# Opening order, the rotary angles' place, and tokens-first layer values in a two-block kernel on one core

## The chip, the core and the metric

The kernel runs on one core of a Trainium2 chip. The metric is the device time of one execution in microseconds (us). TensorE (PE in the profile), VectorE (DVE), ScalarE (ACT), GpSimd (POOL) and SyncE (SP, which here only issues DMAs) each run their own list of instructions in order and meet at semaphores.

## What is computed

The reference is a stack of two models over 512 tokens of width 1024. The first has two layers; each mixes tokens by differential attention and by a gated linear recurrence, followed by an MLP and a gate. The second block (a Mamba layer and an attention layer with 256 context tokens) is not touched by the change except for the names of some semaphores. The part of a first-block layer that matters here:

```python
hn = rms_norm(h, g_mix[l])
proj = hn @ w_in[l]                       # 1024 x 2560
q, k, v, xr, gr = jnp.split(proj, [A, 2 * A, 3 * A, 3 * A + R], axis=-1)
q = partial_rope(q.reshape(B, S, N_DIFF_HEADS, 2, DIFF_HEAD_DIM), positions)
k = partial_rope(k.reshape(B, S, N_DIFF_HEADS, 2, DIFF_HEAD_DIM), positions)
v = v.reshape(B, S, N_DIFF_HEADS, V_HEAD_DIM)
...
o = diff_attention(q, k, v, lam)
xc = causal_depthwise_conv(xr, conv_w[l], conv_b[l])
y = rg_lru(xc, w_gate_a[l], b_gate_a[l], w_gate_x[l], b_gate_x[l], lru_lambda[l])
y = y * jax.nn.gelu(gr)
h = h + jnp.concatenate([o, y], axis=-1) @ w_out[l]
```

## The kernel before

**Weights.** All large weights come as one stream of tiles of 128 x 2048 float32 (1 MB, `wstream`). SP fetches them into two slots `wraw`. GpSimd splits each tile into a rounded high part `whi` (four TENSOR_SCALAR of 128 x 512, line 352) and a rest `wlo` (four TENSOR_TENSOR, line 356). It starts on tile k when tile k has landed and TensorE is done with tile k-2 (semaphore `tile_done`, which starts with two credits), and signals `wsplit`. Tiles 0 and 1 are split "by pieces" (lines 336 and 338): a quarter of `whi`, the same quarter of `wlo`, and a semaphore `w_piece` for each quarter, so that TensorE may begin on a tile that is partly split.

**Products.** `tile()` (line 384) multiplies one tile: for both halves m of its 256 output features and all eight blocks kb of the contraction it issues three products (`whi` by `uhi`, `wlo` by `uhi`, `whi` by `ulo`), where `uhi` and `ulo` are the high part and rest of the activations times the norm's gain. One tile is 48 products of 128 x 512 (line 400). Results stand features by tokens in PSUM. The division by the root mean square is done after the product: VectorE's `mix_out(j)` (line 1642) multiplies tile j's result by `rstd` into `proj`. The layer's ten input tiles are 0, 1 for `xr`, 2, 3 for `gr`, 4, 5 for Q, 6, 7 for K, and 8, 9 for V. A tile's PSUM banks are free again when `mix_out` of the tile two before is done.

**Norm.** ScalarE squares h, VectorE adds (line 1604), TensorE sums over features in the middle of tile 1 (`norm_sum(1)`), ScalarE takes the root, and VectorE the reciprocal (`norm_recip`, line 1612).

**Opening, layer 0.** SP fetches `posi` (positions, one row broadcast to 128 partitions), `misc`, `lpall` (the parameters), and weight tile 0; ScalarE fetches the first half of h, and its second half after the parameters. VectorE waits for the semaphore `cst` (all three of SP's first DMAs), computes the rotary angles (eight instructions, lines 1549 to 1556), one small product, the eight `ulo` blocks (line 1595), the sums of squares, and then `lru_rates`: seventeen instructions on 128 x 4 or 128 x 8 numbers (`softplus` at lines 2353 to 2361 and lines 1579 to 1582), each waiting for the one before. ScalarE has supplied their input (lines 1058 and 1059, after a table load) and takes the sine of the angles after its squares (`rotary`). Then come `norm_recip(1)` and `mix_out(0)`.

**Middle.** VectorE runs mix_out(0), `lambdas` (three small instructions), the convolution of blocks 0 and 1, mix_out(1), blocks 2 and 3, mix_out(2), mix_out(3). TensorE then does the gates' products (line 475), tiles 4 to 7, and the recurrence runs on ScalarE and VectorE beside them, with `mix_out(4)` to `mix_out(7)` in between.

**Values and rotations.** After tile 7 TensorE issues four rotations of Q (`rope`, line 488, a float32 product of a 512-token block with a permutation, two instructions each), tiles 8 and 9, four rotations of K, and then turns V from features by tokens to tokens by features with sixteen 128 x 128 transposes (line 502), since attention needs V as [tokens, features]. VectorE finishes each rotation with three instructions (lines 1711, 1713, 1716). ScalarE copies V to `vtok` (line 1152). The attention loop runs over 16 units of (head, query block): scores on TensorE (lines 517 and 519), maximum on VectorE (line 1736), exponentials on ScalarE (line 1160), `combine` on VectorE (lines 1746 to 1751), transposes and products with V on TensorE. GpSimd meanwhile splits the tile two ahead of the last one finished.

## Time and profile before

| what | value |
|---|---|
| median of the runs | 2647.99 us |
| lowest and highest of three runs | 2640.88 and 2651.42 us |
| the profiled execution's own time | 2651.38 us |
| its span (first to last instruction) | 2649.6 us |
| TensorE busy in it | 2452.4 us, 93% |
| VectorE, GpSimd, ScalarE busy | 54%, 49%, 30% |
| mean granted TensorE clock | 0.963 of full |

The first row is what a change is measured against; the third and fourth belong to the one execution that the trace shows. A share near 93% for TensorE is a busy time with idle gaps around single places, which the views by wait and in order of time show.

### The profile page before, as it was taken

To read this page: it belongs to the slowest core of one execution; us is meant where nothing else is said; L and a number is where in the kernel's file an instruction comes from. 1 tells how busy PE (TensorE), PEld (TensorE's weight loads), DVE (VectorE), ACT (ScalarE), POOL (GpSimd) and SP (SyncE) were. 2 spreads that over 40 slices of the span, in tenths; PEclk is the share of its full clock that TensorE was granted. 3 is DMA by queue.
4 is the path that set the end of the run, shared out by engine and by line. 5 is a ranking of instruction groups with operands and counts; after the bars stand their busy time and mean duration, and the time that the engine had idled before them with its cause. 6 is when DMAs were issued, how large, how long until landed. Compare 5 with 4: busy or idle time off the path is not lost.

```text
span 2649.6 us, 35776 instructions
## 1 busy us (share of the span) xinstructions
PE 2452.4 (93%) x13296; PEld 2042.8 (77%) x13296; DVE 1443.6 (54%) x1778; ACT 798.3 (30%) x1705; POOL 1302.2 (49%) x1204
## 2 busy tenths in 40 slices
PE   6989999999998899999977699999999997998997
PEld 5657888888765688888855688988988886876776
DVE  8564311133766441111336787887888887326762
ACT  2233210112232420011214334334333333325771
POOL 6734766767774276666752243442443431263003
PEclk9989999999998999999998899999999997899999
DMA  4210344343221034434221011111110111121001
GB/s 151 80 48 32 113 142 143 127 135 104 80 80 64 18 104 141 137 129 140 95 102 64 32 49 47 47 39 40 47 47 32 47 54 68 47 81 48 1 1 48
DMA packets 33688, 199.27 MB, mean 75 GB/s; under 512 B 4400, under 2 KB 6576, under 8 KB 13616
## 3 DMA queue, kind: packets, MB, share of 16 engines
q1 hardware_dynamic: 22896, 159.93, 17.5%
q10 hardware_dynamic: 10688, 37.83, 4.4%
q8 instruction: 80, 1.31, 0.2%
q14 instruction: 24, 0.20, 0.0%
HBM read 192.50 MB, written 5.24 MB: 75 GB/s over the span
## 4 chain that ended last, share of the span: by engine, by line
PE 75%; DVE 16%; issue 5%; ACT 3%; POOL 1%; DMA 0%; DVEq 0%; ACTq 0%; SPq 0%; POOLq 0%
PE ps L400 39%; PE ps L653 11%; PE ps L890 5%; DVE convd L1918 3%; PE ps L771 2%; PE ps L749 1%; PE ps L622 1%; PE ps L788 1%; PE ps L971 1%; PE ps L425 1%; PE ps L517 1%; PE ps L988 1%; DVE convd L1932 1%; PE ps L596 1%; PE ps L758 1%
## 5 line engine op out<-in xcount | busy, mean ns | idle before, releaser
L352 POOL TENSOR_SCALAR whi<-wraw 128x512 fp32r<-128x512 f32 x592 | 403.7, 709 | 1312.2 <-PE ps L653 568.8
L356 POOL TENSOR_TENSOR wlo<-wraw,whi 128x512 fp32r<-128x512 f32 x592 | 882.2, 1519 | 0.0
L400 PE MATMUL ps<-uhi,whi 128*128 128x512 f32 x960 | 384.5, 400 | 31.3 <-DVE ulo L1595 16.2
L400 PE MATMUL ps<-uhi,wlo 128*128 128x512 f32 x960 | 377.2, 393 | 0.0
L400 PE MATMUL ps<-ulo,whi 128*128 128x512 f32 x960 | 376.8, 392 | 0.0
L653 PE MATMUL ps<-inhi,whi 128*128 128x384 f32 (+1 forms) x784 | 249.4, 353 | 31.1 <-ACT raw L1291 17.0
L400 PEld LDWEIGHTS ps<-uhi,whi 128*128 128x128 f32 x960 | 182.5, 190 | 78.3 <-issue 28.3
L653 PE MATMUL ps<-inhi,wlo 128*128 128x384 f32 (+1 forms) x784 | 237.6, 338 | 0.0
L653 PE MATMUL ps<-inlo,whi 128*128 128x384 f32 (+1 forms) x784 | 237.4, 338 | 0.0
L1770 DVE TENSOR_TENSOR h<-h,ps 128x1024 f32<-128x1024 f32 x40 | 48.9, 1221 | 307.3 <-PE ps L400 307.3
L400 PEld LDWEIGHTS ps<-uhi,wlo 128*128 128x128 f32 x960 | 182.5, 190 | 38.7 <-issue 1.9
L400 PEld LDWEIGHTS ps<-ulo,whi 128*128 128x128 f32 x960 | 182.2, 190 | 38.6
L400 PE MATMUL ps<-hidhi,whi 128*128 128x512 f32 x512 | 202.2, 395 | 0.0
L400 PE MATMUL ps<-hidhi,wlo 128*128 128x512 f32 x512 | 199.5, 390 | 0.0
L400 PE MATMUL ps<-hidlo,whi 128*128 128x512 f32 x512 | 199.2, 389 | 0.0
L653 PEld LDWEIGHTS ps<-inhi,whi 128*128 128x128 f32 (+1 forms) x784 | 146.1, 190 | 38.4 <-issue 29.5
L1364 ACT ACTIVATE ebuf<-ps,tabg 128x128 f32<-128x128 f32 x384 | 104.2, 383 | 163.5 <-PE ps L760 112.9
L1789 DVE SCALAR_TENSOR_TENSOR hm<-ps,rstd 128x1024 f32<-128x1024 f32 x32 | 39.2, 1224 | 203.2 <-PE ps L400 203.2
L653 PEld LDWEIGHTS ps<-inhi,wlo 128*128 128x128 f32 (+1 forms) x784 | 146.4, 190 | 2.4
L653 PEld LDWEIGHTS ps<-inlo,whi 128*128 128x128 f32 (+1 forms) x784 | 145.8, 189 | 0.9
L1918 DVE SCALAR_TENSOR_TENSOR convd<-raw,cpg,convd 128x770 f32<-128x770 f32 x128 | 142.6, 1114 | 2.3
L1203 ACT ACTIVATE hsq<-hm 128x1024 f32<-128x1024 f32 x32 | 34.0, 1062 | 294.2 <-DVE hm L1789 294.2
(389 smaller groups left out, 4594.8 us busy)
## 6 DMA issues: line engine op xcount, KB each, us to landing
wraw<-in_wstream SPq DMA_DIRECT2D x150, 1024.0 KB, 4.8
modraw<-in_modw ACTq DMA_DIRECT2D x48, 512.0 KB, 3.6
hspill<-hres ACTq DMA_DIRECT2D x1, 3072.0 KB, 8.7
hback<-hspill ACTq DMA_DIRECT2D x1, 3072.0 KB, 10.2
h<-in_x ACTq DMA_DIRECT2D x2, 1024.0 KB, 7.0
out<-hfin SPq DMA_DIRECT2D x2, 1024.0 KB, 3.9
gw<-in_gates ACTq DMA_DIRECT2D x2, 512.0 KB, 4.7
pT<-in_pT ACTq DMA_DIRECT2D x2, 512.0 KB, 4.0
```

Of the source, the lines that this page charges most:

```text
L352: pool.tensor_scalar(whi[:, s, c], wraw[:, s, c], 1.0, 0.0, ALU.mult, ALU.add).then_inc(wraw_read, 1)
L356: ins = pool.tensor_tensor(wlo[:, s, c], wraw[:, s, c], whi[:, s, c].bitcast(F32), ALU.subtract)
L400: mm = pe.matmul(ps[:, 2 * bank + m, :], a[:, w, c:c + P], b[:, kb, :], start=(n == 0 and i == 0), stop=(n == KB - 1 and i == 2))
L425: mm = pe.matmul(ps[32 * j:32 * j + 2, 5, 0:P], cvec[:, kb, :], modraw[:, kb, :], start=(half == 0), stop=(half == 1))
L653: mm = pe.matmul(ps[0:width, q + half, 0:HALF], a[:, s, c:c + width], b[:, kb, half * HALF:(half + 1) * HALF], start=(n == 0), stop=(n == ...
L771: mm = pe.matmul(ps[:, 6, d * 256:(d + 1) * 256], ck[:, c * P:(c + 1) * P], ast[:, slot, :], start=True, stop=True)
L890: mm = pe.matmul(ps[:, q + m, :], a[:, k % 2, c:c + P], b[:, kb, t0:t0 + S], start=(kb == 0 and i == 0), stop=(kb == KB - 1 and i == 2))
L1203: A(hsq[n % 2][:, :, :], hm[n % 2][:, :, :], ACT.Square).then_inc(L["sqh_r"], 1)
L1364: ins = A(ebuf[:, d, r, :], ps[:, 4 + d, r * P:(r + 1) * P], ACT.Exp, bias=tabg[:, K_NB + 2 * c + d, r:r + 1])
L1770: V.tensor_tensor(h[:, 2 * j:2 * j + 2, :], h[:, 2 * j:2 * j + 2, :], TWO(bank), ALU.add).then_inc(L["h_r"], 1)
L1789: V.scalar_tensor_tensor(out=hm[n % 2][:, :, :], in0=TWO(n % 2), scalar=0.0, in1=rstd2, op0=ALU.max, op1=ALU.mult).then_inc(L["m_r"], 1)
L1918: ins = V.scalar_tensor_tensor(out=o, in0=r[:, n:n + CW], scalar=cpg[:, 6 * b + n:6 * b + n + 1], in1=o, op0=ALU.mult, op1=ALU.add)
```

## The change

It has two parts. **Opening:** SP fetches `misc` and `lpall` first and waits for them alone; `posi` comes after weight tile 1, which itself now waits for tile 0 to land; VectorE computes the recurrence's rates (`lru_rates`) before the `ulo` blocks; the angles and the casts of two constants move into layer 0's recurrence, behind line 1688's instruction and ahead of mix_out(5); ScalarE's sines follow there; four weight tiles are split by pieces instead of two. `mix_out(1)` stands ahead of all four convolution blocks, and `lambdas` behind mix_out(3). **Values:** tiles 8 and 9 are multiplied with the activations as the stationary operand and the weights as the moving one, 96 products of 128 x 256 for a tile, so that V comes out tokens first; the sixteen transposes and mix_out(8) and mix_out(9) are gone. As the tokens are now on partitions, `rstd` is needed as a column: `rate_columns` turns it with four one-column products, and ScalarE applies it while it copies V. The rotations are issued in pairs: ahead of tile 8, in its middle, between the tiles, and in the middle of tile 9. The rest of the diff renames semaphores and moves buffers.

```diff
+FIRST = 4
...
     @block.sync
-        sp.dma_start(posi[:, :], io["positions"].partition_broadcast(P)).then_inc(cst, 16)
         sp.dma_start(misc[:, :], io["consts"][:, 256:272]).then_inc(cst, 16)
         sp.dma_start(lpall[:, :, :], io["lparams"]).then_inc(cst, 16)
         sp.dma_start(wraw[:, 0, :], io["wstream"][0]).then_inc(wland[0], 16)
-        sp.wait_ge(cst, CST)
+        sp.wait_ge(wland[0], 16)
         sp.dma_start(wraw[:, 1, :], io["wstream"][1]).then_inc(wland[1], 16)
+        sp.dma_start(posi[:, :], io["positions"].partition_broadcast(P)).then_inc(cst2, 16)
...
     @block.gpsimd
-        for s in range(2):
-            pool.wait_ge(wland[s], 16)
-            pool.wait_ge(tile_done, s + 1)
+        for k in range(FIRST):
+            s = k % 2
+            pool.wait_ge(wland[s], 16 * (k // 2 + 1))
+            pool.wait_ge(tile_done, k + 1)
...
     @block.tensor
-            for m in range(Q0, Q0 + 4):
+            def rate_columns():
+                pe.wait_ge(L["rstd_r"], l * PER["rstd_r"] + 1)
+                pe.wait_ge(L["gate_t"], l * PER["gate_t"] + 8)
+                for t in range(4):
+                    mm = pe.matmul(ps[:, 5, t:t + 1], rstd[:, t * P:(t + 1) * P], ident[:, 0:1], start=True, stop=True)
+                mm.then_inc(L["rcol_ps"], 1)
+
+            def values_tile(j, midway):
+                w = (l * LAYER_TILES + NFM + j) % 2
+                tile_wait(l, NFM + j)
+                banks_wait(j, (L["v_r"], l * PER["v_r"] + 2 * j + 2))
+                for t in range(4):
+                    for kb in range(KB):
+                        for i, (a, b) in enumerate(((uhi, whi), (uhi, wlo), (ulo, whi))):
+                            mm = pe.matmul(ps[:, 2 * j + t // 2, t % 2 * TM:(t % 2 + 1) * TM], a[:, kb, t * P:(t + 1) * P],
+                                           b[:, w, kb * TM:(kb + 1) * TM],
+                                           start=(kb == 0 and i == 0), stop=(kb == KB - 1 and i == 2))
+                    if t == 1:
+                        mm.then_inc(L["v_ps"], 1)
+                        midway()
+                mm.then_inc(tile_done, 1)
+
+            def ropes(m):
                 rope(m)
-            for j in range(8, 10):
-                pair(j)
-            for m in range(K0, K0 + 4):
-                rope(m)
-
-            for t in range(4):
-
-                pe.wait_ge(L["proj_r"], l * PER["proj_r"] + 10)
-                for hd in range(HEADS):
-                    mm = pe.transpose(ps[:, t, hd * P:(hd + 1) * P], proj[:, V0 + hd, t * P:(t + 1) * P], ident[:, :])
-                mm.then_inc(L["v_ps"], 1)
+                rope(m + 1)
+
+            ropes(Q0)
+            rate_columns()
+            values_tile(0, lambda: ropes(Q0 + 2))
+            ropes(K0)
+            values_tile(1, lambda: ropes(K0 + 2))
...
     @block.scalar
-            for t in range(4):
-                act.wait_ge(L["v_ps"], l * PER["v_ps"] + t + 1)
-                A(vtok[:, t, :], ps[:, t, :], ACT.Copy).then_inc(L["v_r"], 1)
+            act.wait_ge(L["rcol_ps"], l * PER["rcol_ps"] + 1)
+            A(small[:, 56:60], ps[:, 5, 0:4], ACT.Copy).then_inc(L["rcol_r"], 1)
+            act.wait_ge(L["rcol_r"], l * PER["rcol_r"] + 1)
+            for j in range(2):
+                for half in range(2):
+                    act.wait_ge(L["v_ps"], l * PER["v_ps"] + j + 1) if half == 0 else tile_wait(NFM + j)
+                    for t in (2 * half, 2 * half + 1):
+                        ins = A(vtok[:, t, j * TM:(j + 1) * TM], ps[:, 2 * j + half, t % 2 * TM:(t % 2 + 1) * TM],
+                                ACT.Copy, scale=small[:, 56 + t:57 + t])
+                    ins.then_inc(L["v_r"], 1)
...
     @block.vector
             if l == 0:
                 lambda_products(0)
+                lru_rates(0)
                 for j in range(4):
                     rest(1, j, C_GMIX)
             for j in range(1, 4):
                 add_squares(1, j, sqn[j - 1])
-            if l == 0:
-                lru_rates(0)
...
             mix_out(0)
-            lambdas()
-            dve.wait_ge(L["proj_r"], l * PER["proj_r"] + 1)
-            conv(0)
-            conv(1)
             mix_out(1)
             dve.wait_ge(L["proj_r"], l * PER["proj_r"] + 2)
-            conv(2)
-            conv(3)
+            for b in range(4):
+                conv(b)
             mix_out(2)
             mix_out(3)
+            lambdas()
...
+            if l == 0:
+                angles()
             mix_out(5)
```

How the order of instructions moves on VectorE, at the very start of the program (`angt` are the angles, `small` the recurrence's parameters; line numbers are those of each kernel). Before:

```order
L1549 CAST angt_109<-posi 128x512
L1550 TENSOR_SCALAR angt_109<-angt_109,misc 128x512
L1551 TENSOR_SCALAR angt_110<-angt_109 128x512
L1552 TENSOR_SCALAR angt_110<-angt_110 128x512
L1554 SCALAR_TENSOR_TENSOR angt_109<-angt_110,angt_109 128x512 x3
L1556 TENSOR_SCALAR angt_109<-angt_109 128x512
L1573 TENSOR_TENSOR small<-lpall 128x2
L1595 SCALAR_TENSOR_TENSOR ulo<-h,lpall,uhi 128x512 x8
L1604 TENSOR_TENSOR acc_66<-acc_66,sqn_94 128x1024
L1604 TENSOR_TENSOR acc_66<-acc_66,sqn_95 128x1024
L1604 TENSOR_TENSOR acc_66<-acc_66,sqn_96 128x1024
```

And of the changed kernel at the same place:

```order
L1605 TENSOR_TENSOR small<-lpall 128x2
L2375 TENSOR_SCALAR small<-small 128x4
L2376 RECIPROCAL small<-small 128x4
L2377 TENSOR_TENSOR small<-small 128x4
...
L2381 SCALAR_TENSOR_TENSOR small<-small 128x4 x6
L2382 SCALAR_TENSOR_TENSOR small<-small 128x4
L2383 TENSOR_SCALAR small<-small 128x4
...
L1614 TENSOR_SCALAR small<-lpall 128x8
L1627 SCALAR_TENSOR_TENSOR ulo<-h,lpall,uhi 128x512 x8
L1636 TENSOR_TENSOR acc_66<-acc_66,sqn_94 128x1024
```

The angles are gone from here, and the seventeen small instructions stand ahead of the `ulo` blocks, on which TensorE's first product waits.

TensorE from the end of tile 7 to attention's first scores; `rperm` marks rotations, `ident,proj` the transposes of V, `proj` alone the scores. Before:

```order
L400 MATMUL ps<-uhi,wlo 128x512
L400 MATMUL ps<-ulo,whi 128x512
L488 MATMUL ps<-proj,rperm 128x512 x4
L400 MATMUL ps<-uhi,whi 128x512
L400 MATMUL ps<-uhi,wlo 128x512
L400 MATMUL ps<-ulo,whi 128x512
...
L400 MATMUL ps<-ulo,whi 128x512
L488 MATMUL ps<-proj,rperm 128x512 x4
L502 MATMUL ps<-ident,proj 128x128 x16
L517 MATMUL ps<-proj 128x128 x2
L519 MATMUL ps<-maskb,identb 128x128 x2
```

Changed (`ident,rstd` are the rate columns, `whi,uhi 128x256` the tokens-first products):

```order
L401 MATMUL ps<-ulo,whi 128x512
L489 MATMUL ps<-proj,rperm 128x512 x2
L496 MATMUL ps<-ident,rstd 128x1 x4
L507 MATMUL ps<-whi,uhi 128x256
L507 MATMUL ps<-wlo,uhi 128x256
L507 MATMUL ps<-whi,ulo 128x256
...
L489 MATMUL ps<-proj,rperm 128x512 x2
...
L489 MATMUL ps<-proj,rperm 128x512 x2
...
L489 MATMUL ps<-proj,rperm 128x512 x2
...
L507 MATMUL ps<-whi,ulo 128x256
L537 MATMUL ps<-proj 128x128 x2
L539 MATMUL ps<-maskb,identb 128x128 x2
```

K's rotations no longer stand behind both value tiles: two pairs of rotations now stand in the middle of a tile's products, and the scores follow the last product of tile 9 directly.

## Rows read from the trace of the kernel before

**Rows 1.** TensorE's waits from 0 to 235 us: total us, times, longest

```profile
...
PE ps L400 <- DVE ulo L1595: 16.2, 1, 16.2
...
PE ps L517 <- DVE proj L1716: 5.2, 1, 5.2
PE ps L400 <- POOL wlo L356: 4.4, 1, 4.4
PE ps L400 <- DVE proj L1642: 4.4, 1, 4.4
```

**Rows 2.** DMA issues from 0 to 30 us: KB each, us from issue to landing

```profile
...
gw<-in_gates ACTq DMA_DIRECT2D x1, 512.0 KB, 3.6
...
posi<-in_positions SPq DMA_DIRECT2D x1, 256.0 KB, 5.9
...
lpall<-in_lparams SPq DMA_DIRECT2D x1, 63.0 KB, 6.0
```

**Rows 3.** ScalarE in order of time, the opening: start us, us, instructions [idle before]

```profile
...
8.12 1.28 ACT L1058 ACT_TABLE_LOAD   x1 [8.12 <-DMA lpall<-in_lparams]
...
9.65 0.20 ACT L1059 ACTIVATE small<-small 128x4 f32<-128x4 f32 x1
...
36.99 0.69 ACT L1095 ACTIVATE rstd<-ps,misc 128x512 f32<-128x512 f32 x1 [10.93 <-PE ps L412]
```

**Rows 4.** VectorE in order of time, the opening

```profile
...
14.90 11.01 DVE L1595 SCALAR_TENSOR_TENSOR ulo<-h,lpall,uhi 128x512 fp32r<-128x512 f32 x8
...
32.66 0.16 DVE L2355 TENSOR_TENSOR small<-small 128x4 f32<-128x4 f32 x1
...
33.05 0.60 DVE L2357 TENSOR_SCALAR small<-small 128x4 f32<-128x4 f32 x1
33.69 5.44 DVE L2359 SCALAR_TENSOR_TENSOR small<-small 128x4 f32<-128x4 f32 x6
...
42.34 3.35 DVE L1612 RECIPROCAL rstd<-rstd 128x512 f32<-128x512 f32 x1
```

**Rows 5.** GpSimd in order of time: the weight splits

```profile
...
10.20 0.68 POOL L336 TENSOR_SCALAR whi<-wraw 128x512 fp32r<-128x512 f32 x1 [9.75 <-DMA wraw<-in_wstream]
...
33.01 2.38 POOL L352 TENSOR_SCALAR whi<-wraw 128x512 fp32r<-128x512 f32 x4 [0.62 <-POOL wlo L338]
35.35 5.01 POOL L356 TENSOR_TENSOR wlo<-wraw,whi 128x512 fp32r<-128x512 f32 x4
...
95.77 5.03 POOL L356 TENSOR_TENSOR wlo<-wraw,whi 128x512 fp32r<-128x512 f32 x4
...
160.03 6.72 POOL L356 TENSOR_TENSOR wlo<-wraw,whi 128x512 fp32r<-128x512 f32 x4
```

**Rows 6.** VectorE in order of time: end of the convolution, and mix_out(5)

```profile
...
60.50 2.78 DVE L1650 SCALAR_TENSOR_TENSOR xc<-proj,lpall,xc 128x511 f32<-128x511 f32 x3
...
102.11 1.23 DVE L1642 TENSOR_TENSOR proj<-ps,rstd 128x1024 f32<-128x1024 f32 x1 [7.37 <-PE ps L400]
```

**Rows 7.** The chain that ended last: full-size products, start us, us

```profile
...
47.10 24.42 PE ps L400 x96
...
135.30 21.79 PE ps L400 x96
```

**Rows 8.** TensorE in order of time: first rotations, first scores

```profile
...
129.82 1.88 PE L488 MATMUL ps<-proj,rperm 128*128 128x512 f32 x4
...
169.37 0.80 PE L517 MATMUL ps<-proj 64*128 64x128 f32 x4 [5.24 <-DVE proj L1716]
```

**Rows 9.** The chain that ended last: tokens-first products of the second block

```profile
...
2289.34 17.27 PE ps L872 x144
```

**Rows 10.** Line 846: one-column float32 products, ns min/median/max, first and last start

```profile
...
L846 PE MATMUL ps<-ones,sq x96: 165/352/352, 2246.2 to 2262.6; 128*128 128x1 f32 x96
```

**Rows 11.** VectorE in order of time: the last rotation, the fourth score maximum

```profile
...
167.22 0.68 DVE L1711 SCALAR_TENSOR_TENSOR rtmp<-ps,ropeS 128x512 f32<-128x512 f32 x1
...
176.58 1.23 DVE L1736 TENSOR_REDUCE small<-ps 128x2 f32<-128x1024 f32 x1 [0.53 <-PE ps L519]
```

More of the change, by code:

```diff
@@ L46 @@
 NLP = 63
-XR, GR, Q0, K0, V0 = 0, 4, 8, 12, 16
+XR, GR, Q0, K0 = 0, 4, 8, 12
+NFM = 8
 CTX = 256
```

95 lines of the change are left out of this document (45 added, 50 removed).

## The prediction

> **What bounds the kernel now.** I read the page of the profile first: TensorE is busy 93% of the span (the table above), so only time in which it stands idle, or work of its own, is worth anything. The view of TensorE's waits over the first 235 us then names the places in layer 0: 16.2 us until the first `ulo` block, 5.2 us before attention's first scores until the last rotation is added, 4.4 us on GpSimd's split of tile 7, and 4.4 us on `mix_out(0)` [rows 1]. Layer 1 has the same wait before the scores. Third, the timelines show what is late at each. In the opening VectorE sits until `lpall` has landed at 7.7 us [rows 2, 3], then spends the time to 14.90 on the angles and one small product before the first `ulo` [rows 4]; later TensorE awaits `mix_out(0)`, because the small instructions of `lru_rates` still run when the root is done (36.99 + 0.69, [rows 3]), and the reciprocal starts only at 42.34 [rows 4]. Ahead of attention all four rotations of K and the transposes follow tile 9: from the first rotation at 129.82 to the first scores at 169.37 are 39.6 us [rows 8], of which VectorE's last rotations are the end.
>
> **The cost of VectorE beside GpSimd** decides both parts. The small instructions take 0.16 us alone (line 2355, [rows 4]) but 0.60 while GpSimd runs `whi` and, inside the six of line 2359, up to 1.2 us while it runs `wlo`: from 33.05 on VectorE finished eight small instructions in just the 7.4 us in which GpSimd ran its eight [rows 4, 5]. So beside a split each small VectorE instruction costs one GpSimd instruction, 0.92 us on average, and about 1.0 where the split goes by pieces and has gaps; alone about 0.2 with its semaphore. The Trainium skill (page "SBUF — State Buffer", section "Who interferes with whom") says the same as a rule: VectorE with two SBUF inputs, or in a two-port mode, and GpSimd take their shared port pair in turn, each for a whole instruction. By that rule the move of the rates to where GpSimd begins its first tile speaks against the change, and it prices them as the rows do, at one GpSimd instruction each; were there no such turn-taking, the opening below would gain 7 us instead of 1.4.
>
> **Values, for each of two layers.** TensorE's new work between tile 7 and the scores: eight rotations, 1.88 us for two [rows 8], 7.5 us; 192 products of 128 x 256, for which the second block's tokens-first tile is the same form, 17.27 us for 144, 0.120 us each [rows 9], 23.0 us; four one-column products, eight instructions at 0.17 us start to start (16.4 us for 95) [rows 10], 1.4 us. Sum 31.9. The products themselves get dearer, 23.0 for 21.8 us [rows 7]; what is saved are the transposes, the waits within the rotations, and above all the tail. Is VectorE in time? The last rotation takes it 2.1 us with GpSimd idle (167.22 to the scores at 169.37, [rows 8, 11]); beside a split, where each of the two instructions without PSUM may wait for one of GpSimd's, I estimate 3.3. The last two are issued in the middle of tile 9, 5.8 us of products before its end, when the split of the next tile is nearly over: 4.1 to 6.6 us of work, so it ends 1.7 us before to 0.8 us after TensorE; I take 0.3 us of cost. ScalarE's last copies of V and a table load (1.28 us, [rows 3]) now follow the last product; the first exponentials can start some 2.2 us behind the scores' start, about when the first maxima are there. Gross gain: 39.6 - 31.9 = 7.6, less 0.3.
>
> What comes back: GpSimd's split of tile 11 starts when tile 9 is done. Before, it ran out under the last rotations (until 166.8, [rows 5]) and attention had GpSimd idle. Now tile 9 ends where the scores start, so about 7.4 us of split lie on attention's first units. `combine` of unit 0 has three instructions that take from SBUF, and each waits for a `wlo` (5.01 / 4 = 1.25 us) where it ran in 0.2 to 0.35: 2.7 us. The fourth maximum, which started 7.2 us behind the first scores (176.58 - 169.37, [rows 8, 11]), had waited 0.53 for TensorE [rows 11]; that much is slack. So 2.1 us; if the maxima, which read PSUM, and the reciprocals are blocked too it is 4; below it is 0, if GpSimd is the one who yields. The same section of the Trainium skill has reductions never contend; by it the 2.1 stand, and no row here shows it either way. Net per layer 7.6 - 0.3 - 2.1 = 5.2, bounds 3 and 7.6. Two layers: 10.4, from 6 to 15.
>
> **Opening.** Behind TensorE's first product at S come tiles 0 and 1 with the norm's sum (26.4 us, up to 42.7), then the 4.4 us wait, then tiles 2 and 3 in 24.42 us, where the same 96 products take 21.79 elsewhere: 2.6 us for slow products after the idle time [rows 1, 7]. With the rates gone from between, the norm's chain is: the root at S + 20.8 (36.99 - 16.2) and 0.7 long, reciprocal 3.4 [rows 3, 4], mix_out(0) 1.2, thus S + 26.1, before tile 1 ends. Both the 4.4 and the 2.6 go: 7.0 us gained, if S stays at 16.2. But S moves. `lpall` landed at 1.67 + 6.0 = 7.7, `posi` at 0.75 + 5.9 = 6.65 ahead of it in the same queue [rows 2]. Without `posi` it lands between 4.8 (issued at 1.2, and 3.6 us, the quickest landing in the opening, [rows 2]) and 7.2 (as long as before); I take 5.8. ScalarE then needs 2.1 us (7.7 to 9.85, [rows 3]) for the rates' input: 7.9. GpSimd began at 10.20 when weight tile 0 had landed [rows 5]; with 256 KB less ahead of it I put it at 9.0. About five of the seventeen instructions run free, twelve beside the split at 1.0: the rates end near 20.7, the first `ulo` (1.2 us there) at 21.8. S is 5.6 later and the opening gains 7.0 - 5.6 = 1.4 us. With `lpall` at 4.8 nearly eleven run free and S is near 16 (gain 7); with 7.2 all are beside the split and S is near 26 (loss 3). Weight tile 1 is fetched only after tile 0 has landed; GpSimd needs it 8 us later, the fetch takes about 7: nothing. Splitting tiles 2 and 3 by pieces lets TensorE start early on them, but tile 2's split (S + 13.3 to S + 21.5) and tile 3's first piece are ready anyway: nothing.
>
> **Moved work taken as hidden.** The angles with one small product took 7.2 us in the opening (7.7 to 14.9), partly beside a split [rows 2, 4]; they go into 7.37 us in which VectorE awaited tile 5 [rows 6]; GpSimd's `wlo` of tile 6 runs there (95.77 to 100.8, [rows 5]) and would end about 1 us later, 0.5 before it is needed; mix_out(5) up to 3 us later, which frees a bank for tile 7, 10 us on. The recurrence behind it shifts by as much, on whose overlap the 4.4 us wait for tile 7's split rests; I charge 0.3. Without that cover the angles would cost 3 us. The four convolutions in a row behind mix_out(1) end 1 to 2 us ahead of tile 3 by my count of turns, where they had 8 us of room (60.50 + 2.78 against 47.10 + 24.42, [rows 6, 7]): nothing, but each us beyond is one on the gates. ScalarE's sines with their table load lie in its wait for the scan.
>
> **Sum.** 10.4 + 1.4 - 0.3 = 11.5 us; as S has more room below than above I round to 12.5. The profiled execution took 2651.38 us, 3.4 above the median of the runs; off the median that makes 2635.5 us.
>
> **Rivals.** (a) *Both parts run free of GpSimd*: the parameters land near 4.8 and attention is not held up. For it: without `posi` only 71 KB stand ahead of the weights. Against it: the small instructions and the splits take turns plainly [rows 4, 5]. 7 + 15 = 22 us, 2626. (b) *The rates cost all that they free*: S at 26, opening loses 3 us, values at the low end or 5 each: 3 to 8 us, 2642. For it: `lpall`'s landing may hang on the fetch of h, which is as large as before. (c) *Slower:* the loading of the stationary operand sets the pace, since a layer now loads 192 of them for 96. If a 128 x 256 product takes the 0.227 us of a 128 x 512 one (21.79 / 96, [rows 7]), a layer pays 192 x 0.107 = 20.6 us more; the sum turns into 29 us lost, 2677. It decides, for 0.5% slower, from 0.18 us on. Against it stands the same form in the same kernel [rows 9]. (d) *No effect:* the waits merely change their name (attention's start held by the last rotation instead, 5 us, and S later by 7): 2647.
>
> **Chances.** Forecast (gain 8 to 17) 0.50, (a) 0.22, (b) 0.18, (c) 0.03, (d) 0.07. A measurement of this kernel tells about 0.5%, 13.2 us, from no change. Of the forecast's 0.50 half lies beyond that, and (a): faster 0.47. The other half, (d), and (b) but for 0.02: same 0.48. (c), and 0.02 of (b) where the angles or convolutions come out dearer besides: slower 0.05. Range: from just below (a), 2622, to (b)'s upper side, 2646; this leaves out a little of (a), and (c) and (d), some 0.15. It is as wide as the two unknown bounds (S, and attention beside the split) make it.
>
> **What the profile after will show.** TensorE's first product at 21.8 us (16: the rates ran free; 26: none did), and small VectorE instructions of about 1 us beside GpSimd's pieces. No wait of TensorE on mix_out(0). Tokens-first products 0.12 us apart. First scores 32 us behind tile 7's end in both layers, and line 1736's fourth maximum 9 us behind them, with GpSimd's `wlo` beside. A wait of the gates on the convolution, or of tile 6 or 7 on a later split than before, would make the forecast too good.

## The result, and the profile after

The changed kernel takes 2627.42 us (median of 6 executions, 2622.64 to 2629.79), the kernel before 2644.94 on the same chip (6 executions, 2640.26 to 2652.94): 0.9927 of it, 95% interval 0.9908 to 0.9947. It is faster by 17.5 us, 0.7%, where 12.5 were forecast, in a band of 8 to 17. The forecast time, 2635.5, was counted from the 2647.99 known then, and the measured one is 8.1 below it: 5.0 for the larger gain, 3.1 because the median before came out lower with more executions. The profiled execution of after took 2622.64 us, span 2620.8, granted clock 0.969.

The view of TensorE's waits over the first 235 us, to be laid beside [rows 1]:

```profile
...
PE ps L401 <- DVE ulo L1627: 18.1, 1, 18.1
PE ps L547 <- DVE patt L1777: 7.9, 6, 2.3
...
PE ps L537 <- ACT pexp L1188: 2.0, 3, 1.2
...
PE ps L401 <- POOL wlo L357: 0.2, 1, 0.2
```

and of before, two lines of the same view on the waits inside attention:

```profile
...
PE ps L527 <- DVE patt L1751: 5.6, 5, 2.1
...
PE ps L517 <- ACT pexp L1160: 0.8, 2, 0.4
```

The wait on mix_out(0) is gone (L401 <- DVE proj), as forecast. The 4.4 us wait for tile 7's split is down to 0.2, which was not. The 5.2 us before the scores is gone. Inside attention the waits have grown, from 5.6 to 7.9 us on `patt` and from 0.8 to 2.0 on `pexp`. The first product waits 18.1 us; 21.8 were forecast.

The opening, in order of time, ScalarE, GpSimd, VectorE, to be laid beside [rows 3 to 5]:

```profile
...
6.40 1.28 ACT L1078 ACT_TABLE_LOAD   x1 [6.40 <-DMA lpall<-in_lparams]
...
7.93 0.20 ACT L1079 ACTIVATE small<-small 128x4 f32<-128x4 f32 x1
```

```profile
...
8.55 0.62 POOL L337 TENSOR_SCALAR whi<-wraw 128x512 fp32r<-128x512 f32 x1 [8.10 <-DMA wraw<-in_wstream]
9.26 1.27 POOL L339 TENSOR_TENSOR wlo<-wraw,whi 128x512 fp32r<-128x512 f32 x1
10.49 0.62 POOL L337 TENSOR_SCALAR whi<-wraw 128x512 fp32r<-128x512 f32 x1
```

```profile
...
8.17 0.17 DVE L2375 TENSOR_SCALAR small<-small 128x4 f32<-128x4 f32 x1 [1.90 <-ACT small L1079]
...
8.59 0.59 DVE L2377 TENSOR_TENSOR small<-small 128x4 f32<-128x4 f32 x1
9.21 0.16 DVE L2378 TENSOR_TENSOR small<-small 128x4 f32<-128x4 f32 x1
9.41 1.14 DVE L2379 TENSOR_SCALAR small<-small 128x4 f32<-128x4 f32 x1
10.59 3.83 DVE L2381 SCALAR_TENSOR_TENSOR small<-small 128x4 f32<-128x4 f32 x6
...
17.23 10.54 DVE L1627 SCALAR_TENSOR_TENSOR ulo<-h,lpall,uhi 128x512 fp32r<-128x512 f32 x8
...
39.63 3.35 DVE L1644 RECIPROCAL rstd<-rstd 128x512 f32<-128x512 f32 x1 [8.07 <-ACT rstd L1115]
```

`lpall` landed 4.8 us after its issue at 1.2, and ScalarE's table load starts at 6.40 instead of 8.12. The seventeen small operations of the rates run from 8.17 to 17.3. GpSimd does one piece in 1.94 us (8.55 to 10.49), and VectorE gets about three small instructions into it: one stretched to 0.59, one free at 0.16, one stretched to 1.14, and so on. VectorE then stands idle for 8.07 us before the reciprocal at 39.63.

The middle of layer 0, VectorE and GpSimd, where before had mix_out(5) behind 7.37 us of idle time [rows 6]:

```profile
...
89.55 0.84 DVE L1579 CAST angt<-posi 128x512 f32<-128x512 int32 x1
...
100.37 1.23 DVE L1668 TENSOR_TENSOR proj<-ps,rstd 128x1024 f32<-128x1024 f32 x1
101.51 3.40 DVE L1717 TENSOR_TENSOR xc<-gt,xc 128x2048 f32<-128x2048 f32 x1
104.94 7.34 DVE L1720 TENSOR_TENSOR_SCAN asq<-ga,xc 128x512 f32<-128x512 f32 x4
```

```profile
...
97.22 3.03 POOL L353 TENSOR_SCALAR whi<-wraw 128x512 fp32r<-128x512 f32 x4 [0.37 <-PE ps L401]
100.22 8.00 POOL L357 TENSOR_TENSOR wlo<-wraw,whi 128x512 fp32r<-128x512 f32 x4
```

The angles and two casts fill 89.55 to 100.3. The scans start at 104.94. By then the `whi` half of tile 7's split is over; it took 3.03 us, where before it took 5.31, from 102.27, beside the product ahead of the scans (103.25) and the first of them (105.65). The split is done at 108.2.

To follow the gain through the program I use six points that every kernel passes: TensorE's first rotation, its first scores, and the first product on `osq` (attention's end), in layers 0 and 1. One profiled execution of each kernel (us; `e5` and `e9` are explained below):

| kernel | rot. 0 | scores 0 | end 0 | rot. 1 | scores 1 | end 1 | span |
|---|---|---|---|---|---|---|---|
| before | 129.8 | 169.4 | 214.1 | 800.9 | 840.4 | 886.4 | 2649.6 |
| e5, before again | 129.8 | 169.4 | 214.1 | 801.0 | 840.5 | 886.4 | 2646.2 |
| e9, semaphores merged | 130.8 | 170.4 | 213.1 | 797.9 | 837.4 | 878.7 | 2641.9 |
| after | 119.3 | 150.9 | 197.7 | 783.7 | 814.5 | 859.9 | 2620.8 |
| e1, values only | 130.0 | 160.8 | 207.0 | 792.2 | 823.0 | 868.4 | 2632.9 |
| e2, opening only | 121.3 | 165.1 | 207.6 | 793.6 | 833.2 | 877.9 | 2640.8 |
| e3, rates last | 114.4 | 146.0 | 191.7 | 777.6 | 808.5 | 853.8 | 2621.5 |
| e4, positions first | 121.0 | 152.6 | 199.1 | 787.5 | 818.3 | 865.4 | 2632.3 |
| e6, angles earlier | 127.5 | 158.4 | 205.6 | 792.8 | 823.7 | 870.2 | 2634.5 |
| e7, scans held | 121.2 | 152.8 | 198.4 | 778.7 | 812.3 | 860.6 | 2623.4 |
| e8, split held | 119.0 | 150.6 | 196.6 | 783.9 | 814.8 | 858.8 | 2625.2 |
| e10, e3 and e8 | 116.2 | 147.8 | 190.1 | 776.1 | 806.9 | 850.2 | 2613.1 |
| e11, e10 and two more | 116.2 | 147.8 | 191.9 | 770.4 | 802.5 | 846.1 | 2610.5 |
| e12, and the table early | 116.1 | 147.7 | 190.5 | 769.5 | 803.1 | 845.9 | 2610.2 |

### The profile page after: what moved, and what is told of

Its sections match the earlier page's. It is cut to its first block, busy times and chain, and to the rows that moved or that the text cites. A ratio compares the mean times of both kernels' runs of the same rounds, so it can differ in the third digit from the quotient of the medians.

```text
span 2620.8 us, 36134 instructions
## 1 busy us (share of the span) xinstructions
PE 2438.6 (93%) x13472; PEld 2044.4 (78%) x13472; DVE 1454.4 (55%) x1774; ACT 801.7 (31%) x1715; POOL 1301.9 (50%) x1204
## 4 chain that ended last, share of the span: by engine, by line
PE 75%; DVE 14%; issue 5%; ACT 3%; POOL 1%; DMA 0%; DVEq 0%; ACTq 0%; SPq 0%; POOLq 0%
PE ps L401 37%; PE ps L673 11%; PE ps L910 5%; DVE convd L1943 3%; PE ps L791 2%; PE ps L507 2%; PE ps L769 1%; POOL wlo L357 1%; PE ps L642 1%; PE ps L808 1%; PE ps L426 1%; PE ps L991 1%; PE ps L1008 1%; DVE convd L1957 1%; PE ps L616 1%
## 5 line engine op out<-in xcount | busy, mean ns | idle before, releaser
L401 PE MATMUL ps<-uhi,whi 128*128 128x512 f32 x896 | 356.6, 398 | 24.5 <-DVE ulo L1627 18.1
L401 PE MATMUL ps<-uhi,wlo 128*128 128x512 f32 x896 | 350.4, 391 | 0.0
L401 PE MATMUL ps<-ulo,whi 128*128 128x512 f32 x896 | 350.1, 391 | 0.0
L401 PEld LDWEIGHTS ps<-uhi,whi 128*128 128x128 f32 x896 | 169.2, 189 | 67.9 <-issue 24.9
L401 PE MATMUL ps<-hidhi,whi 128*128 128x512 f32 x512 | 202.1, 395 | 0.0
L401 PE MATMUL ps<-hidhi,wlo 128*128 128x512 f32 x512 | 199.5, 390 | 0.0
L401 PE MATMUL ps<-hidlo,whi 128*128 128x512 f32 x512 | 199.2, 389 | 0.0
L401 PEld LDWEIGHTS ps<-ulo,whi 128*128 128x128 f32 x896 | 169.1, 189 | 35.8
L401 PEld LDWEIGHTS ps<-uhi,wlo 128*128 128x128 f32 x896 | 169.3, 189 | 35.5 <-issue 1.4
```

The costliest lines, as they stand in the source:

```text
L401: mm = pe.matmul(ps[:, 2 * bank + m, :], a[:, w, c:c + P], b[:, kb, :], start=(n == 0 and i == 0), stop=(n == KB - 1 and i == 2))
```

## The experiments

**The two halves apart (e1, e2).** `e1` has before's opening, convolution order and angles, and the new values; `e2` the other way round.

```diff
 # e1, against after
-FIRST = 4
+FIRST = 2
-                lru_rates(0)
...
+            if l == 0:
+                lru_rates(0)
...
-            if l == 0:
-                angles()
```

> The opening and the order of the middle as before, the values tokens-first as after. Theory (the trace after, segment by segment): the first part of both layers is untouched, so that the first product stands at 16.2 us, mix_out(3) of layer 0 ends near 71.5 and TensorE waits 4.4 us for tile 7's split in layer 0 too; the stretch from the first rotation to the first scores falls by about 8 in each layer and attention gives 1 to 2 back in layer 0: 6 to 7 us in layer 0, 7 to 9 in layer 1, a time 13 to 16 us under before's (about 2630). Rival 1 (my prediction's term): 10.4 us. Rival 2: the values bring next to nothing by themselves and the gain seen came from the opening: under 4 us.

> The opening, the conv order and the moved angles as after, the values as before (ten feature tiles, turned by TensorE). Theory: mix_out(3) of layer 0 at 66.4 us (5.1 earlier), the wait for tile 7's split in layer 0 gone (about 5 us more, because VectorE's angles push the scans past that split's first half), the wait in layer 1 still 4.4 us, and 1 us given back at the gates of layer 1: 8 to 10 us under before's time. Rival 1 (my prediction's terms): 1.1 us, the wait of layer 0 stays. Rival 2: the wait of layer 0 moves to the next split and only 5 us are left. If both this and the values-only kernel hold their theory, their gains add up to the whole change's 17.5 within 5 us.

Measured: `e1` 2635.92 us, ratio 0.9964 (0.9948 to 0.9980), 6.9 us in medians; `e2` 2643.55, ratio 0.9994 (0.9979 to 1.0010). Together 6, not 17.5. The points of the table say where the sum fails. `e1` has every wait of the old opening:

```profile
...
PE ps L401 <- DVE ulo L1621: 16.2, 1, 16.2
...
PE ps L401 <- POOL wlo L357: 4.4, 1, 4.4
PE ps L401 <- DVE proj L1668: 4.3, 1, 4.3
```

and its values segments are 30.8 and 30.8 us against 39.6 and 39.5. `e2` reaches the first rotation 8.5 us ahead of before, but the stretch to the scores is 43.8 us instead of 39.6. In it TensorE waits (columns: us, times, longest):

```profile
...
PE ps L518 <- DVE proj L1715: 5.2, 1, 5.2
PE ps L489 <- DVE rtmp L1710: 3.9, 4, 2.1
```

The same window of before has 2.7 us on `rtmp` and the same 5.2. So 1.2 us of the 4.2 are waits for VectorE. Layer 1 of e2, which has no angles, waits 2.7 us on `rtmp` as before does, so it is the angles that make VectorE late for layer 0's rotations. The rest is the granted clock. This view by stretch (start and end, length, busy times of PE, PEld, DVE, ACT and POOL, granted clock, DMA) shows before and then e2:

```profile
...
129.80:169.40 39.60, 31.67 (x131) 22.40 (x129) 25.26 (x27) 3.35 (x5) 26.40 (x24) 0.98 0.24 83
```

```profile
...
121.30:165.10 43.80, 34.75 (x129) 23.75 (x127) 27.91 (x29) 3.35 (x5) 30.09 (x26) 0.90 0.22 80
```

TensorE is busy 3.1 us longer with the same products, at 0.90 of the clock instead of 0.98. In after the values' products stand between the pairs of rotations and VectorE catches up behind them: 31.6 us. The halves are not independent: the new values cover the lateness that the new opening makes. Measured against e9, the kernel before in an execution near its median (explained below), the account closes. Up to attention's end in layer 0 (213.1 in e9) e1 gains 6.1 and e2 5.5, and with the 4.2 that e2 alone pays that makes 15.8; after gains 15.4. Up to attention's end in layer 1 they gain 10.3 and 0.8; with the 4.2, and 3.4 us by which e2's attention there is longer than e9's (44.7 for 41.3, at a granted clock of 0.81 for 0.93), that makes 18.7; after gains 18.8.

**Rates behind the squares again (e3), positions ahead of the parameters again (e4).**

```diff
 # e3
                 lambda_products(0)
-                lru_rates(0)
...
             for j in range(1, 4):
                 add_squares(1, j, sqn[j - 1])
+            if l == 0:
+                lru_rates(0)
             norm_recip(1)
 # e4
+        sp.dma_start(posi[:, :], io["positions"].partition_broadcast(P)).then_inc(cst2, 16)
         sp.dma_start(misc[:, :], io["consts"][:, 256:272]).then_inc(cst, 16)
```

> After, with the decay rates computed behind the opening's squares, as before the change, and all else kept. Theory: the first ulo block comes earlier (8 to 12 us), but the rates stand again between the last square and the norm's reciprocal; they are 17 small operations without a split beside them, 5 to 7 us in all, so mix_out(0) waits longer again (TensorE waits 2 to 5 us for it) and mix_out(3) of layer 0 ends 1 to 4 us later than after's 66.4: the whole is 0 to 4 us slower than after. Rival: what is computed first or last makes no difference, because the opening is bound by weight loads and splits (products of tile 3): mix_out(3) within 0.5 us of 66.4.

> After, with the broadcast of the positions issued ahead of the parameters again, nothing else moved. Theory: the parameters land 1.5 to 2 us later (7.7 us, as before), ScalarE's table load and exponentials and GpSimd's first split start that much later (8.1, 9.7, 10.2), the rates run later beside the split, so the first product stands at 19.5 to 22 and mix_out(3) of layer 0 ends 1.5 to 3 us later than 66.4. Rival: the rates take what room the split leaves them and the first ulo comes where it comes in after (18.1 within 0.5); the order of the issues is worth nothing.

`e3` went against its theory and its rival: its first rotation comes 4.9 us earlier than after's, mix_out(3) of layer 0 at 61.53 instead of 66.43, and attention's end in layer 1 is 6.1 us earlier. The median, 2624.26 us (2622.76 to 2627.77), is 3.2 below after's, a difference within the spread of both, and the traced execution's span, 2621.5, is no shorter than after's 2620.8; so for the whole program the gain is not shown by this run alone. Its waits and its VectorE in the opening:

```profile
...
PE ps L401 <- POOL wlo L339: 10.9, 1, 10.9
PE ps L401 <- DVE proj L1669: 2.9, 1, 2.9
```

```profile
...
24.84 1.25 DVE L2376 TENSOR_SCALAR small<-small 128x4 f32<-128x4 f32 x1
...
28.08 2.85 DVE L2382 SCALAR_TENSOR_TENSOR small<-small 128x4 f32<-128x4 f32 x6
...
34.33 0.55 DVE L1614 TENSOR_SCALAR small<-lpall 128x8 f32<-128x8 f32 x1
34.78 3.34 DVE L1644 RECIPROCAL rstd<-rstd 128x512 f32<-128x512 f32 x1
```

The rates cost 10 us there too (24.84 to 34.9, seventeen instructions at 0.59 on average, beside a split that now goes by pieces; beside the whole split of before eight of them took 0.92 each [rows 4, 5]). But they lie in the time in which after's VectorE stood idle for 8.07 us and waited for the root, and so add only 2.9 us to TensorE's wait, while rates placed first add 7.2 to the first one (18.1 against 10.9). Up to the first rotation, rates first is thus a piece of the change that costs time. `e4` held in the opening: the first product waited 20.1 us instead of 18.1, mix_out(3) and the first rotation came 1.7 later. Its median is 2630.95 us (2626.93 to 2634.07), ratio 0.9938; its spread overlaps after's.

**Which execution is before's? (e5, e9).** With the points of before's first profile, e1 had gained 18 us at the end of layer 1 and e2 8.5, about 10 more than their medians. `e5` is the kernel before, unchanged, executed once more with the profiler on (2647.96 us).

> The kernel before once more, for a second profile. Measured so far: the two halves of the change alone give 6.9 and -0.7 us in medians, while the milestones of their profiles against before's first profile say 18 and 8.5. Theory: the first profile of before caught an execution with a low granted clock (0.963; most executions of before stand at 0.970 and near 2641 us, some at 0.964 and 2652), and the difference lies in stretches at half clock in layers 0 and 1 that other executions don't have: at 0.970 the first rotation of layer 0 stands at 126 to 130 us and the attention of layer 1 ends at 876 to 882 instead of 886.4. Rival: the stretches lie behind layer 1, in the second block; then the milestones of layers 0 and 1 are as in the first profile within 1 us and what follows is shorter by about 9.

Neither held in full: the points were those of the first profile to 0.1 us, as the rival had it, but behind them only 3.4 us were missing and not 9. `e9` then asked whether the merged semaphores, which all variants share with after, are what they pay for:

```diff
-                ins.then_inc(in_v, 1)
-                act.wait_ge(in_v, KB * i + b + 1)
+                st(ins)
...
-            V.tensor_copy(tabg[:, :, :], tab[:, :, bass.ds(g * HPG, HPG)]).then_inc(tabg_r, 1)
-            dve.wait_ge(tabg_r, g + 1)
+            k(V.tensor_copy(tabg[:, :, :], tab[:, :, bass.ds(g * HPG, HPG)]))
```

> The kernel before with one edit of the change alone: in the second block four semaphores are merged into others (same waits, same order, no instruction added or taken). Measured so far: at the end of layer 1's attention the change's profile is 26.5 us ahead of before's two profiles, but the medians differ by 15 to 17.5 only, and every variant that shares the merged semaphores lacks 8 to 10 us in the same way. Theory (clock: the second block's stretches at half clock differ from execution to execution, and before's fall more lucky on average): the merge costs nothing, ratio to before 1.000 with an interval that holds 1.0, median within 3 us of before's. Rival: the merged semaphores cost the second block 8 to 10 us: ratio 1.003 to 1.004.

They cost nothing that can be measured: 2643.37 us, ratio 0.9992 (0.9977 to 1.0007). And this profile, of the instructions of before in layers 0 and 1, caught another kind of execution: attention of layer 1 took 41.3 us instead of 46.0. The view by stretch of e5, e9 and after, layer 1's attention:

```profile
...
840.00:886.00 46.00, 38.12 (x215) 24.88 (x216) 32.10 (x81) 26.95 (x86) 0.00 (x0) 0.80 0.05 21
```

```profile
...
837.00:879.00 42.00, 34.32 (x217) 21.54 (x218) 31.93 (x81) 27.07 (x87) 0.00 (x0) 0.93 0.05 21
```

```profile
...
815.00:860.00 45.00, 34.55 (x215) 22.58 (x214) 34.02 (x80) 28.66 (x89) 7.12 (x8) 0.89 0.08 24
```

VectorE and ScalarE are busy equally long in the first two; the granted clock is 0.80 in one and 0.93 in the other, and TensorE's same products are busy 38.1 us in one and 34.3 in the other. Of 50 executions of before in these comparisons 30 had a mean clock of 0.967 or more and a median of 2642.0 us, the other 20 lay below it with 2652.2. Both profiles of the unchanged kernel are of slower granted clock (0.963, 0.966) than its median execution; e9 at 2643.66 us is one like the median. Against it after's attention is *longer*: 46.8 for 42.7 in layer 0, 45.4 for 41.3 in layer 1. From after to e9 are 18.8 us at the end of layer 1, where before's first profile had made it 26.5; the difference of 7.7 is what the profiles had too much, for e1 and e2 as well. 6.7 of it lie in the two attentions (44.7 for 42.7 and 46.0 for 41.3).

**Why layer 0's wait for tile 7's split went (e6), and layer 1's (e7).** `e6` puts `angles()` ahead of mix_out(4), in a single execution (2636.28 us); `e7` adds one wait, in layer 1 only.

```diff
 # e7
             mix_out(5)
+            if l:
+                dve.wait_ge(wsplit, l * LAYER_TILES + 8)
```

> After, with the angles one product-drain earlier on VectorE: ahead of mix_out(4) instead of behind the gate's operation (and ScalarE's sine and cosine unmoved in its own order). Theory: in after the angles pushed layer 0's scans behind the first half of tile 7's split, which is why TensorE's 4.4 us wait for that split is gone in layer 0 and stands in layer 1; here they start at 83 us, mix_out(5) is back in idle time, the scans start at 97 to 100 and meet the whole split of tile 7: TensorE waits 2 to 4.4 us for it in layer 0 again, the first rotation stands at 122 to 125 us instead of 119.3, layer 1 unchanged. Rival: the wait went for another reason (the earlier tiles): layer 0's wait stays under 0.5 us and the first rotation at 119 to 120.

> After, and in layer 1 alone VectorE waits, before it multiplies xc and scans, until GpSimd has split tile 7. Theory (they share a resource and stretch each other: the split took 15.1 us beside the scans and takes 9.2 to 9.5 alone): the split ends near 765.6 instead of 771.2, TensorE's 4.4 us wait for it in layer 1 goes, with it the stretch at half clock behind it; the scans start at 766 and the last of VectorE's chain (oylo, mix_out(7)) is late by 0 to 4 us for the rotations, which the values' products cover in part: layer 1 shorter by 2 to 5 us. Rival: VectorE's chain sets the pace; mix_out(7) is as late as the wait was long, the first rotations wait for it, and layer 1 gains nothing or loses up to 4 us.

`e6`: the wait is back, 4.4 us. The first rotation is at 127.5, later than forecast, since the clock also fell to half (1.2 of 2.4 GHz) for 3.4 us at 71 and for 6.8 us at 112, behind the wait, where after's profile has no such stretch before 156. GpSimd's tile 7 beside the scans of that run:

```profile
...
99.28 5.31 POOL L353 TENSOR_SCALAR whi<-wraw 128x512 fp32r<-128x512 f32 x4 [1.26 <-PE ps L401]
104.57 9.77 POOL L357 TENSOR_TENSOR wlo<-wraw,whi 128x512 fp32r<-128x512 f32 x4
```

15.1 us, where after's took 11.0. The angles are the same work in both; what differs is whether they keep the scans behind the `whi` half. So it was the angles' place, not their cost, that took layer 0's wait away. `e7`: in layer 1 the wait is 0, the first rotation comes 5.0 us earlier than in after, and both engines run at their own pace:

```profile
...
764.69 2.29 DVE L1719 TENSOR_TENSOR xc<-gt,xc 128x2048 f32<-128x2048 f32 x1 [6.34 <-POOL wlo L357]
767.02 5.31 DVE L1722 TENSOR_TENSOR_SCAN asq<-ga,xc 128x512 f32<-128x512 f32 x4
```

```profile
...
757.29 2.38 POOL L353 TENSOR_SCALAR whi<-wraw 128x512 fp32r<-128x512 f32 x4 [1.47 <-PE ps L401]
759.63 5.03 POOL L357 TENSOR_TENSOR wlo<-wraw,whi 128x512 fp32r<-128x512 f32 x4
```

The scans take 5.31 us instead of 7.33, the split 7.4 instead of 15.1. But the end of layer 1's attention is where it was (860.6 for 859.9), and the median (2625.14, from 2623.74 to 2625.67) is only 2.3 lower, within after's spread. The next split is 1.1 us late for TensorE and 3.4 us of the values run at half clock, which makes that segment 33.6 us instead of 30.8; attention is 48.3 us long instead of 45.4, with 18.7 us of it at half clock where after has 10.2. Neither the theory's sum nor the rival's cause: the rotations were not late. Whether the hold itself brings the lower clock is not shown; `e11` below has the same hold, and its attention in layer 1 ran at 0.92.

**What attention pays (e8, e12).** `e8` withholds the release of tile 11's split until attention's last product.

```diff
-                mm.then_inc(tile_done, 1)
+                mm.then_inc(L["v_ps"] if j else tile_done, 1)
...
             values(N - 1)
+            pe.wait_ge(L["v_ps"], l * PER["v_ps"] + 3)
+            pe.sem_inc(tile_done, 1)
```

> After, with GpSimd's split of tile 11 held until the attention's last product, in both layers (tile 11 is needed 22 us after that). Theory: the split runs beside the first four score blocks and stretches VectorE's maxima and combines (1.25 us for a 128x128 scaling instead of about 0.2); without it the fourth maximum stands 7.2 us behind the first scores instead of 9.4, and attention is 1.5 to 2.5 us shorter in layer 0 and 0.5 to 2.5 in layer 1; the time is 2 to 5 us under after's. Rival: attention is bound elsewhere (ScalarE's exponentials and TensorE's turns) and its length does not change by over 0.5; or the split, held, meets the norm at the attention's end and takes the gain back there.

In after, layer 1, GpSimd and VectorE stand so behind the first scores (814.5):

```profile
...
814.81 2.37 POOL L353 TENSOR_SCALAR whi<-wraw 128x512 fp32r<-128x512 f32 x4 [5.83 <-PE ps L507]
817.14 4.98 POOL L357 TENSOR_TENSOR wlo<-wraw,whi 128x512 fp32r<-128x512 f32 x4
```

```profile
...
818.46 1.25 DVE L1776 TENSOR_SCALAR patt<-pexp,small 128x128 f32<-128x128 f32 x1
819.75 1.25 DVE L1777 SCALAR_TENSOR_TENSOR patt<-pexp,small,patt 128x128 f32<-128x128 f32 x1
820.92 0.94 DVE L1762 TENSOR_REDUCE small<-ps 128x2 f32<-128x768 f32 x1
...
823.90 1.23 DVE L1762 TENSOR_REDUCE small<-ps 128x2 f32<-128x1024 f32 x1 [0.85 <-PE ps L539]
```

and in e8 (first scores 814.8):

```profile
...
818.28 0.28 DVE L1781 TENSOR_SCALAR patt<-pexp,small 128x128 f32<-128x128 f32 x1
818.60 0.35 DVE L1782 SCALAR_TENSOR_TENSOR patt<-pexp,small,patt 128x128 f32<-128x128 f32 x1
819.08 0.96 DVE L1767 TENSOR_REDUCE small<-ps 128x2 f32<-128x768 f32 x1
```

The two operations on `patt` take 0.28 and 0.35 instead of 1.25 each, and the fourth maximum starts 6.3 us behind the scores (9.4 in after; 6.7 in e9). A maximum reads PSUM and is not stretched beside the split (0.94 beside it, 0.96 without). TensorE's waits on `patt` fall from 7.9 to 6.4 us in layer 0 and to 5.9 in layer 1. Attention is only 0.8 and 1.4 us shorter, less than forecast, but its granted clock is a little lower too. So I put its length beside the time in which TensorE was busy in it:

| attention | layer 0: us, TensorE busy, clock | not busy | layer 1: us, TensorE busy, clock | not busy |
|---|---|---|---|---|
| e9 | 42.7, 35.82, 0.88 | 6.9 | 41.3, 34.02, 0.93 | 7.3 |
| after | 46.8, 36.48, 0.85 | 10.3 | 45.4, 34.95, 0.89 | 10.4 |
| e8 | 46.0, 37.19, 0.84 | 8.8 | 44.0, 35.66, 0.88 | 8.3 |
| e11 | 44.1, 35.72, 0.88 | 8.4 | 43.6, 34.46, 0.92 | 9.1 |
| e12 | 42.8, 34.45, 0.92 | 8.4 | 42.8, 34.44, 0.92 | 8.4 |

Holding the split takes 1.5 and 2.1 us out of the time in which TensorE is not busy. Of the 4.1 us by which after's attention is longer than e9's, 0.7 and 0.9 are longer busy times at a lower clock. This division is an estimate, since the ends of products are modelled in the trace. The median of e8, 2622.53 us (2617.47 to 2627.03), is not clear of after's spread.

`e12` (on top of e11, below) computes one exponential of a single column between the two values tiles:

```diff
                     ins.then_inc(L["v_r"], 1)
+                if j == 0:
+                    A(small[:, 60:61], small[:, 56:57], ACT.Exp)
```

> The previous kernel (rates last, split of tile 11 held, layer 1's scans held, layer 1's convolutions in before's order) with one exponential of a single column on ScalarE between the first and the second values tile, so that the exponential's table is loaded there and not behind the last value copy. Theory: at the same granted clock attention is 4.1 us longer in after than in before for two reasons: tile 11's split (taken away already) and ScalarE, whose last two value copies and table load of 1.28 us now stand behind the first scores; the first exponential comes 0.7 us nearer to the first scores (1.6 instead of 2.3), attention is 0.5 to 1.5 us shorter in each layer, the median 1 to 3 us below 2611.1. Rival: ScalarE is not what the first turn waits for, attention keeps its length within 0.3 at the same clock.

ScalarE at the first scores (147.7):

```profile
...
147.81 0.84 ACT L1183 ACTIVATE vtok<-ps,small 128x256 f32<-128x256 f32 x2 [6.63 <-PE ps L507]
148.91 0.37 ACT L1195 ACTIVATE pexp<-ps,small 128x128 f32<-128x128 f32 x1 [0.26 <-DVE small L1776]
```

No table load stands between the last value copy and the first exponential any more; the latter starts 1.2 us behind the scores (2.3 in after and e11). The waits on `pexp` fall from 2.0 to 0.8 us, attention from 44.1 and 43.6 to 42.8 and 42.8. Layer 1's 0.8 is at the same clock and the same busy time (the table above); layer 0's 1.3 is all busy time, at 0.92 instead of 0.88. The expectation set out from attention being 4.1 us longer "at the same granted clock" in after; it was not the same, 0.85 and 0.89 against e9's 0.88 and 0.93. The median, 2609.67 against 2611.12, leaves the gain of the whole unproven. The end of layer 1's attention (845.9 for 846.1) shows nothing left of it; e12 has 3.4 us at half clock in the stretch of the values ahead of it and e11 none.

**Together (e10, e11).** `e10` is e3 and e8; `e11` adds e7's wait and, in layer 1, before's order of convolutions.

> After, with the rates behind the squares again (as in the run that did that alone) and the split of tile 11 held until the attention's end in both layers. Theory: the two gains lie at different places and add up: first rotation of layer 0 at 114.4 us (4.9 earlier than after), layer 1's attention ended at 852 to 853 (after 859.9), a median of 2617 to 2622. Rival: the later stages give it back (the granted clock), median 2622 to 2627 with the same milestones.

> The previous kernel with two more edits in layer 1 alone: VectorE holds the scans until tile 7 is split, and the convolutions in before's order (two behind mix_out(0), two behind mix_out(1)). Theory: layer 1's wait for tile 7's split (4.4) gone, the gates' wait 1.3 instead of 1.9 and mix_out(2) earlier by 1; first rotation of layer 1 near 767 to 769, the attention's end at 846 to 850, median 2 to 6 us under the previous kernel's. Rival: as with the hold alone the attention runs at a lower granted clock behind it and takes back what the hold gave: end of layer 1's attention at 851 to 853, the same time as the previous kernel.

`e10`: 2617.79 us, ratio 0.9896 (0.9873 to 0.9919), end of layer 1 at 850.2; the theory's median held, though the first rotation stood at 116.2 instead of 114.4 (half clock for 3.4 us at 40). `e11`: 2611.12 us, ratio 0.9866 (0.9839 to 0.9892), the end at 846.1; the first rotation of layer 1, at 770.4, missed its 767 to 769, and the median is 6.7 under e10's where 2 to 6 were expected. The gates' wait in layer 1 is 1.3 instead of 1.9, and the wait for tile 7's split is gone. The rival, a lower clock in attention behind the hold, did not come. Both are faster than after beyond its spread (their slowest executions took 2621.16 and 2612.25, after's fastest 2622.64); with e12 (0.9861, 0.9834 to 0.9888) they are the best versions.

## Why the prediction was right, and where it was not

The forecast of a moderate gain held and the time lies in the range, but the sum of 11.5 was made of terms that erred in both directions, and that they partly offset each other is luck. The time is even nearer to rival (a)'s 2626 than to the forecast's 2635.5, but not by its mechanism: the first product stood at 18.1 and not at 16, and attention was held up. Values and attention are measured here against e9, whose execution is like the median one, the opening and the angles against before's first profile. The segments from e9 to after are 11.5 + 8.0 - 4.1 - 1.2 + 8.7 - 4.1, and 2.3 behind layer 1, together 21.1, which is the 21.0 us between these two executions. After's profile is 4.8 us better than its own median, and e9's is 0.3 above its own, so some 4 of the 21.1 belong to these two executions and not to the kernels. In which segments they lie is not shown, as after was traced once; the granted clock of attention, above, worked against after.

- **Values, gross 7.6 less 0.3.** Right: 8.0 and 8.7. First scores 31.6 and 30.8 us behind the first rotation (forecast 32), products 0.12 us apart. The weight loads do not set the pace: rival (c) needed more than 0.18 us for a product.
- **Attention, -2.1 per layer.** Right in what it priced, short as a sum: -4.1. Tile 11's split, the whole of the 2.1, is 1.5 and 2.1 us of it by e8. The table load, which I saw and took to be ready "about when the first maxima are there", was put at nothing and is 0.8 by e12 in layer 1. Another 0.7 and 0.9 are busy time at a lower granted clock. With split and table load both out of the way (e12), TensorE is still not busy for 1.1 to 1.5 us more than in e9; that is unassigned. The fourth maximum behind the scores by 9.4 us was forecast at 9.
- **Opening, 1.4.** Mis-sized: mix_out(3) came 5.1 us earlier (71.55 to 66.43; 4.7 against e9). The step that failed is "twelve beside the split at 1.0". The split and the small instructions do hold each other up, but three of these fit in a piece of two GpSimd instructions: fifteen took 8.7 us, 0.58 each. The 1.0 came from a whole split [rows 4, 5], and I had it rise, not fall, for one by pieces. `lpall` landed at 6.0, as taken (5.8). Thus S, TensorE's first product, was at 18.1, not 21.8, and these 3.7 us are the surplus of 5.1 over 1.4. The Trainium skill (page "SBUF — State Buffer", section "Who interferes with whom") has the shared port pair held for a whole instruction and reductions free of it; the reduction's rows agree (0.94 beside the split, 0.96 without). The rows of the small ones show some blocked and some not; whether the slow ones were blocked for their two SBUF inputs or for a two-port mode, the two forms that the prediction names, no run separates.
- **What the opening's reordering is worth.** The prediction took the rates to be well placed in front, as the only question was how many run free. e3 shows that they stood better where they were, by 4.9 us at the first rotation: the time between the last square and the root is idle on VectorE and holds most of them.
- **Moved angles, -0.3.** Wrong in sign: the prediction let the 4.4 us wait for tile 7's split stand and charged 0.3 for the shift of the scans. Measured is +5.4 (10.5 us gained at the first rotation, 5.1 by the opening), 4.2 of it this wait in layer 0. Before also has 3.4 us at half clock behind the wait, at 117, and after none. I had mix_out(5) "up to 3 us later", but did not carry it to GpSimd: the `whi` half of tile 7's split then ran before the scans. e6 shows it by moving the angles alone, layer 1 by having none.
- **Convolutions in a row, 0.** They cost 1.0 us in layer 1: from the reciprocal to mix_out(4) are 49.2 us in before and 50.2 in after, and the gates wait 1.9 instead of 1.3. In e11, with the old order, it is 49.2 and 1.3 again.

The halves' medians do not add up to the whole for two reasons, both above: the new values cover VectorE's lateness (4.2 us in e2), and e2's attention in layer 1 ran at half clock for 17.4 us of its 44.7. The traced execution of e2 (2642.61) is near the median of its twelve (2643.55), but how the clock lay in the others is open.

## What to carry to other kernels

A piece of work that two engines dislike to do together has a place as well as a price: placing VectorE's scans 4 us later against GpSimd's split took a wait of 4.4 us away. Before moving work ahead for an early start, look for idle time later on the same engine: the rates belonged in the wait for the root, not ahead of everything. And when a profile is compared, compare its own time and granted clock with its kernel's median first; two profiles of before agreed to 0.1 us at every point and were both slower than the kernel's median.

## What was not expected of the hardware

- The same instructions (layer 1 of e5 and of e9) run at a granted clock of 0.80 or 0.93 over layer 1's attention, a stretch in which TensorE often waits, and take 46.0 or 41.3 us. That is 4.7 us in this one stretch. For the whole kernel, executions of before at a mean clock of 0.967 or more have a median of 2642.0 us and the others 2652.2. In e7 a gain of 5.0 us at the first rotation was gone at attention's end, which ran at 0.81 instead of after's 0.89; e11, with the same hold and the old order of convolutions, was 5.7 us ahead of e10 at that rotation and still 4.1 ahead at attention's end, at 0.92. What decides between these no run here shows.
- Scans and splits stretch each other, the split most: side by side 7.33 and 15.1 us, apart 5.31 and 7.4.
- Beside a split by pieces (0.62 and 1.27 us by turns) small VectorE instructions took 0.58 us on average in after and 0.59 in e3, beside a whole one 0.92 in before.
